# A second norm applied in two places, its feature weights by quarter beside the output products and its token factor at scores and Gelu

## The chip, the cores and the metric

The program runs on one core of one Trainium2 chip. The metric is the time of one execution in microseconds on the device; lower is better. The kernel before was run three times: median 2408.66 us, from 2407.15 to 2410.4.

## What is computed

A stream `x` of 256 tokens by 1024 features goes through one block with a conventional feed-forward part and then through two layers of a second kind. The change is in those two layers only. One such layer is:

```python
def rms_norm_2(x, g):
    y = xf * lax.rsqrt(jnp.mean(xf * xf, axis=-1, keepdims=True) + EPS)
    return (y * g.astype(jnp.float32)).astype(x.dtype)

x = x + token_mixer(rms_norm_2(x, norm_mix[l]), ...)      # ends with merged @ w_out
x = x + peer_ffn(rms_norm_2(x, norm_ffn[l]), ...)

def chunk(xc):                                             # in peer_ffn
    q = (xc @ w_query).reshape(PEER_CHUNK, PEER_HEADS, 2, half)
    s = jnp.einsum('thpk,pnk->thpn', q, sub_keys)
    sv, si = lax.top_k(s, PEER_TOPK)
...
    g = jax.nn.softmax(top_s, axis=-1)
    u = expert_down[eidx]
    vv = expert_up[eidx]
    act = jax.nn.gelu(jnp.einsum('td,thkd->thk', xc, u), approximate=False)
    return jnp.einsum('thk,thkd->td', (g * act), vv)
```

The normed stream `xc` is used twice: in the query product, whose result is scored against 128 keys per side, and in the dot products with 128 chosen expert rows per token (8 heads, 16 each). Both uses are linear in it up to the scores and up to the Gelu.

## The kernel before, in words

**Products.** All weights stream through a ring of three slots (`weights`, L884 on SyncE's queue), in halves of 512 KB. A half is split into a high part by ScalarE (`split_hi`, L443) and a low part by VectorE (`split_lo`, L448); the features are split likewise (`feat_hi`, `feat_lo`, called FH and FL). A product is then three matmuls (`product`, L463 to L465). `split_hi` of half n + 3 waits until half n's products are done (`half_done`), and the load of a slot waits for `split_lo` of what was in it. One half is eight products, 24 matmuls; a group is two halves and 256 output columns.

**The layers of the second kind** are a loop of two turns on each engine, with the instructions written in the same order on each turn. After attention and the two branch products come the four groups of output products (`wo_pe`, WO = 4). Their eight halves stand in the order `WO_ORDER`: group 0 and 1 first by feature half, then groups 2 and 3. I number these halves 0 to 7. As each group is done, VectorE adds it to its quarter of the stream `x` (L1501).

**The norm before the queries** (`n_peer`) then runs as a chain over four engines. ScalarE loads the table with the root (L316) and sums the squares of the first three quarters (`squares_act`, L324), then of the last (`norm_act`, L335), and takes the root (L340). VectorE forms mean and reciprocal (L348, L352, L356) and multiplies the stream by token factor and feature weights into `h_norm`, called HN (L366). TensorE, which runs 28 products with zeros meanwhile to stay busy (`keep_warm(pe, 7)`, L403), transposes HN in 16 blocks (`norm_pe`, L410); ScalarE copies each bank to FH (L390), VectorE subtracts to FL (L373).

**The queries and keys.** Eight query groups follow (`group_fm`, L_PQ = 8), each copied by ScalarE to `pqT` (L1294) and scored (`key_scores`, L1064); ScalarE copies the scores of one head to `SC` in one instruction (`take_scores`, L1286). VectorE finds the top 16 of 16 by pieces: `keyed` and `paired`, for the first head written between the weight splits of the query groups, up to the indices (L1569).

**The experts.** POOL issues a gather of 1 MB for each of 256 picks per layer into a ring of eight slots (L930). For each, VectorE takes the dot product with HN (L1612), ScalarE takes Gelu (L1313), multiplies by the gate (L1315) and forms a diagonal (L1318), and TensorE accumulates (L1085) and frees the slot.

What sets the order around the change is each engine's written order alone, with these semaphores: `half_done`, `wo_taken` (a bank of output products is read), `x_ready`, and of the norm `hn` (HN ready), `xp` (transposed), `hi` and `hT` (feature parts ready).

## Time and profile before

| | |
|---|---|
| median of 3 runs | 2408.66 us |
| profiled execution | 2412.3 us |
| its span, first to last instruction | 2410.5 us |
| granted TensorE clock, mean | 0.98 |
| TensorE busy | 2107.4 us (87%) |
| VectorE busy | 1640.8 us (68%) |
| ScalarE busy | 1113.4 us (46%) |
| POOL busy | 822.3 us (34%) |
| read from memory | 708.29 MB, 296 GB/s over the span |

The profiled execution is one more run than the three, with 1.8 us around its span. Busy time is a mean over stages that have different limits, so the stage has to be looked at: output products, norm and query products of layer 1 lie between 765 and 855 us, its gathers between 841 and 1490; in layer 2 the same begins near 1680. Of each wait the profile names the engine and line that released it.

### The profile page before, as it was taken

What the parts mean: (1) busy time and instruction counts of PE and PEld (TensorE: products, weight loads), DVE (VectorE), ACT (ScalarE), POOL (GpSimd) and SP (SyncE); (2) the same over time, 40 slices, a digit from 0 to 9 for tenths busy, and PEclk for the clock granted to TensorE, in tenths of its full rate; (3) what the DMA queues carried; (4) which work ended last, traced back from release to release, by engine and by line L of the source; (5) the groups of instructions that cost most, each with busy time, mean ns of one, the idle gap of its engine ahead of it and who ended that gap; (6) DMA issues with size and microseconds to landing.
All of it is one profiled execution on the core that took longest, in us unless ns stands there. A gap on an engine that the chain in (4) does not pass through costs nothing.

```text
span 2410.5 us, 32536 instructions
## 1 busy us (share of the span) xinstructions
PE 2107.4 (87%) x10192; PEld 1383.8 (57%) x10246; DVE 1640.8 (68%) x3313; ACT 1113.4 (46%) x2532; POOL 822.3 (34%) x562
## 2 busy tenths in 40 slices
PE   8999999999999988878877787999987877878877
PEld 7899899998999842222322222999852222322222
DVE  3555777777766577777777775776567777777776
ACT  5344455555544444444444444544444444444443
POOL 0000011100100066655666662010056566665663
PEclk9999999999999999999999998999999999999999
DMA  7333456655533499999999997433489999999998
GB/s 257 123 116 126 143 163 196 204 190 188 166 109 130 132 420 422 422 422 422 421 421 422 422 422 317 167 114 110 136 349 422 422 422 422 422 422 422 422 422 345
DMA packets 122844, 710.66 MB, mean 295 GB/s; under 512 B 14161, under 2 KB 16721, under 8 KB 56582
## 3 DMA queue, kind: packets, MB, share of 16 engines
q0 software_dynamic: 75264, 540.05, 54.1%
q1 hardware_dynamic: 43600, 159.12, 20.0%
q10 hardware_dynamic: 3894, 10.35, 1.2%
q8 instruction: 54, 0.88, 0.2%
q14 instruction: 32, 0.26, 0.0%
HBM read 708.29 MB, written 4.32 MB: 296 GB/s over the span
## 4 chain that ended last, share of the span: by engine, by line
PE 46%; DMA 31%; issue 7%; ACT 6%; DVE 5%; POOL 5%; POOLq 0%; ACTq 0%; DVEq 0%
DMA work<-in_experts,expert_idx 31%; PE ps L463 11%; PE ps L465 11%; PE ps L464 11%; PE ps L1085 6%; POOL work L930 5%; DVE work L1612 2%; PE ps L543 2%; PE ps L578 2%; PE ps L556 1%; ACT arena L1318 1%; ACT small L1315 1%; ACT L1313 1%; DVE weights_lo L448 1%; PE ps L1064 1%
## 5 line engine op out<-in xcount | busy, mean ns | idle before, releaser
L1085 PE MATMUL ps<-work,arena 128*128 128x512 f32 x2048 | 1017.2, 629 | 250.5 <-ACT arena L1318 248.9
L930 POOL DMA_INDIRECT work<-in_experts,expert_idx x512 | 778.9, 1521 | 843.7 <-issue 554.6
L1085 PEld LDWEIGHTS ps<-work,arena 128*128 128x128 f32 x2048 | 365.9, 194 | 900.1 <-ACT arena L1318 592.5
L1612 DVE CUSTOM_DVE_ANT_0 work<-h_norm,work 128x1024 f32<-128x1024 f32 x512 | 629.9, 1230 | 338.5 <-DMA work<-in_experts,expert_idx 332.0
L448 DVE TENSOR_TENSOR weights_lo<-weights,weights_hi 128x1024 fp32r<-128x1024 f32 x298 | 367.2, 1237 | 220.6 <-ACT weights_hi L443 220.4
L443 ACT ACTIVATE weights_hi<-weights 128x1024 fp32r<-128x1024 f32 x298 | 314.3, 1057 | 383.5 <-PE ps L465 363.8
L463 PE MATMUL ps<-feat_hi,weights_hi 128*128 128x256 f32 x1576 | 452.8, 287 | 7.6 <-DVE feat_lo L376 4.1
L464 PE MATMUL ps<-feat_lo,weights_hi 128*128 128x256 f32 x1576 | 447.5, 284 | 0.0
L465 PE MATMUL ps<-feat_hi,weights_lo 128*128 128x256 f32 x1576 | 447.3, 284 | 0.0
L1313 ACT ACTIVATE small<-small 128x1 f32<-128x1 f32 x512 | 103.7, 203 | 666.8 <-DVE small L1612 666.2
L463 PEld LDWEIGHTS ps<-feat_hi,weights_hi 128*128 128x128 f32 x1576 | 304.1, 193 | 12.1 <-issue 7.2
L464 PEld LDWEIGHTS ps<-feat_lo,weights_hi 128*128 128x128 f32 x1576 | 304.3, 193 | 0.6
L465 PEld LDWEIGHTS ps<-feat_hi,weights_lo 128*128 128x128 f32 x1576 | 303.9, 193 | 0.0
L1318 ACT ACTIVATE arena<-consts,small 128x128 f32<-128x128 f32 x512 | 205.6, 402 | 16.7
L904 POOL DMA_DIRECT2D na_rows<-in_rpb x32 | 21.2, 662 | 467.0 <-PE ps L465 467.0
L463 PE MATMUL ps<-weights_hi,feat_hi 128*128 128x256 f32 (+1 forms) x560 | 164.3, 293 | 7.0 <-DVE feat_lo L749 5.3
L1315 ACT ACTIVATE small<-small,expert_gate 128x1 f32<-128x1 f32 x512 | 150.7, 294 | 16.6
L464 PE MATMUL ps<-weights_lo,feat_hi 128*128 128x256 f32 (+1 forms) x560 | 158.2, 282 | 0.0
L465 PE MATMUL ps<-weights_hi,feat_lo 128*128 128x256 f32 (+1 forms) x560 | 158.0, 282 | 0.0
L463 PEld LDWEIGHTS ps<-weights_hi,feat_hi 128*128 128x128 f32 x560 | 107.4, 192 | 8.3 <-issue 4.4
L464 PEld LDWEIGHTS ps<-weights_lo,feat_hi 128*128 128x128 f32 x560 | 107.2, 191 | 0.7
L465 PEld LDWEIGHTS ps<-weights_hi,feat_lo 128*128 128x128 f32 x560 | 107.2, 191 | 0.0
(174 smaller groups left out, 1785.1 us busy)
## 6 DMA issues: line engine op xcount, KB each, us to landing
weights<-in_wstream SPq DMA_DIRECT2D x298, 512.0 KB, 3.6
work<-in_experts,expert_idx POOLq DMA_INDIRECT x512
na_rows<-in_rpb POOLq DMA_DIRECT2D x32, 96.0 KB, 4.0
arena<-na_rows ACTq DMA_DIRECT2D x2, 1536.0 KB, 10.7
params<-in_par ACTq DMA_DIRECT2D x2, 1476.0 KB, 7.3
work<-bias_rows ACTq DMA_DIRECT2D x3, 512.0 KB, 6.6
params<-in_par ACTq DMA_DIRECT2D x1, 1156.0 KB, 11.7
x<-in_x SPq DMA_DIRECT2D x1, 1024.0 KB, 5.0
```

The costliest lines, as they stand in the source:

```text
L443: nc.scalar.activation(WH[:, n % SLOTS, :], W[:, n % SLOTS, :], ACT.Copy).then_inc(w_hi, 1)
L448: nc.vector.tensor_tensor(WL[:, n % SLOTS, :], W[:, n % SLOTS, :], WH[:, n % SLOTS, :], ALU.subtract).then_inc(w_lo, 1)
L463: nc.tensor.matmul(out, stat[0], mov[0], start=start, stop=False)
L464: nc.tensor.matmul(out, stat[0], mov[1], start=False, stop=False)
L465: return nc.tensor.matmul(out, stat[1], mov[0], start=False, stop=stop)
L543: ins = nc.tensor.matmul(ps[:, at:at + k.shape[-1]], q, k, start=True, stop=True)
L930: nc.gpsimd.indirect_dma_start(ring[:, r, :], None, experts, bass.IndirectOffsetOnAxis(ap=EIDX[:, b, c * RING + r:c * RING + r + 1], axis= ...
L1085: ins = nc.tensor.matmul(bank(2 * t + h), DIAG[:, r, :], ring[:, r, D + h * 512:D + (h + 1) * 512], start=False, stop=False)
L1313: nc.scalar.activation(ga[:, r:r + 1], hd[:, r:r + 1], ACT.Gelu).then_inc(gelu_ready, 1)
L1315: nc.scalar.activation(gw8[:, r:r + 1], ga[:, r:r + 1], ACT.Copy, scale=GWT[:, b, c * RING + r:c * RING + r + 1]).then_inc(w_ready, 1)
L1318: nc.scalar.activation(DIAG[:, r, :], ident, ACT.Copy, scale=gw8[:, r:r + 1]).then_inc(diag_ready, 1)
L1612: nc.vector.tensor_tensor_reduce(ring[:, r, 0:D], HN[:, t, :], ring[:, r, 0:D], 1.0, 0.0, ALU.mult, ALU.add, hd[:, r:r + 1]).then_inc(dots ...
```

## The change

In the loop of the two layers, the norm's two factors are taken apart. The feature weights are multiplied in by VectorE quarter by quarter, right after each quarter of the sum (so HN is now the stream times the feature weights, without the token factor). TensorE transposes quarters 0, 1 and 2 after halves 4, 5 and 6 of the output products, and quarter 3 inside the first query half, after its fourth chunk; the keep-warm products and `norm_pe` go. ScalarE copies the transposed banks 0 and 1 after half 6 and banks 2 and 3 after half 7, since FH and FL still hold the merged features until then. The squares are summed over whole rows afterwards, into `Y` instead of HN; root and reciprocal follow. The token factor `rstd` enters as a per-token scale when the scores are copied (now one instruction per 128 tokens, L1313 of the changed kernel) and as the scale of Gelu.

```diff
--- before.py
+++ after.py
@@ -759,7 +759,15 @@
             split_lo(dve, 2 * (g0 + BR) - 1 + SLOTS, at)
             lower(BR - 1)
 
-        def wo_pe(pe, gates, g0, l=0, at=0):
+        def turned_pe(pe, nm, l, g):
+
+            pe.wait_ge(nm.hn, 4 * l + g + 1)
+            for c in (2 * g, 2 * g + 1):
+                for t in range(TT):
+                    ins = nc.tensor.transpose(ps[:, c * S + t * P:c * S + (t + 1) * P], HN[:, t, c * P:(c + 1) * P], ident)
+            ins.then_inc(nm.xp, 1)
+
+        def wo_pe(pe, gates, g0, l=0, at=0, turned=None):
 
 
             done = 0 if isinstance(l, int) else l * BR + BR
@@ -770,6 +778,8 @@
                     pe.wait_ge(wo_taken, g - 1 if isinstance(l, int) else l * (WO - 1) + WO + g - 1)
                 half_tok(pe, 2 * g0 + n, 6 + g % 2, h, at,
                          also=(lambda c: c % 2 or pe.wait_ge(mt_lo, done + c // 2 + 1)) if g == 0 else None)
+                if turned and n in (4, 5, 6):
+                    turned_pe(pe, turned, l, n - 4)
 
         def wo_done(g):
 
@@ -1049,10 +1059,7 @@
                     else:
                         values_pe(pe, AT2, what[1], l)
                 branches_pe(pe, AT2, fill_o2, G_LAYER + LG_BR, PARTS2, l, at)
-                wo_pe(pe, (lproj_taken, l * N2 + L_PROJ + L_GATE), G_LAYER + LG_WO, l, at)
-
-                keep_warm(pe, 7)
-                norm_pe(pe, n_peer, l)
+                wo_pe(pe, (lproj_taken, l * N2 + L_PROJ + L_GATE), G_LAYER + LG_WO, l, at, turned=n_peer)
 
                 def key_scores(h):
 
@@ -1066,11 +1073,17 @@
                                                    PAR[:, Q_KEYS + s * NKEY:Q_KEYS + (s + 1) * NKEY], start=True, stop=True)
                     ins.then_inc(sc_done, 1)
 
+                def normed(c):
+
+                    if c == 4:
+                        turned_pe(pe, n_peer, l, 3)
+                    if c % 2 == 0:
+                        pe.wait_ge(n_peer.hT, l * 4 + c // 2 + 1)
+
                 for j in range(L_PQ):
                     if j >= 2:
                         pe.wait_ge(lproj_taken, l * N2 + L_PROJ + L_GATE + j - 1)
-                    group_fm(pe, G_LAYER + LG_PQ + j, 6 + j % 2, at, also=(
-                        lambda c: c % 2 or pe.wait_ge(n_peer.hT, l * 4 + c // 2 + 1)) if j == 0 else None)
+                    group_fm(pe, G_LAYER + LG_PQ + j, 6 + j % 2, at, also=normed if j == 0 else None)
                     if j != 1:
                         key_scores(max(j - 1, 0))
                 key_scores(PH - 1)
@@ -1268,13 +1281,25 @@
                         heads_parts(nc.scalar, AT2, what[1].fill + what[1].copies, l, range(EARLY))
                 gates_act(2 * KC, (lproj_taken, l * N2 + L_PROJ + L_GATE))
                 merge_act(act, AT2, fill_o2, G_LAYER + LG_BR, l, at)
-                for n in range(2 * LG_WO, 2 * LG_PQ):
-                    split_hi(act, L_HALF + n + SLOTS, at)
-                root_table(303)
-                squares_act(act, stream, (wo_taken, l * (WO - 1) + WO + WO - 1))
+                wo_halves = at.halves + L_HALF + 2 * LG_WO
+                for n in range(2 * WO - 2):
+                    split_hi(act, L_HALF + 2 * LG_WO + n + SLOTS, at)
+                    if n == 3:
+                        root_table(303)
+                for b in range(4):
+                    if b in (0, 2):
+                        act.wait_ge(half_done, wo_halves + 2 * WO - 1 + b // 2)
+                    act.wait_ge(n_peer.xp, 4 * l + b + 1)
+                    nc.scalar.activation(two(FH, b), bank(b), ACT.Copy).then_inc(n_peer.hi, 1)
+                    if b == 1:
+                        split_hi(act, L_HALF + 2 * LG_PQ + 1, at)
+                split_hi(act, L_HALF + 2 * LG_PQ + 2, at)
                 act.wait_ge(x_ready, l * 3 + 2 * TT + 1)
-                norm_act(act, n_peer, stream, l, first=EARLY_D)
-                norm_act_hi(act, n_peer, l, None)
+                for t in range(TT):
+                    ins = nc.scalar.activation(Y[:, t, :], X[:, t, :], ACT.Square, accum_out=ssq[:, t:t + 1])
+                ins.then_inc(n_peer.sq, 1)
+                act.wait_ge(n_peer.var, l + 1)
+                nc.scalar.activation(std, ssq, ACT.Sqrt).then_inc(n_peer.std, 1)
 
                 def gate_exp(k):
 
@@ -1283,8 +1308,11 @@
 
                 def take_scores(h):
                     act.wait_ge(sc_done, l * PH + h + 1)
-                    nc.scalar.activation(SC[:, 0:STEPS, :, :].rearrange("p (t h) s n -> p t h (s n)", h=PH)[:, :, h, :],
-                                         bank(4 + h % 2).rearrange("p (t n) -> p t n", t=TT), ACT.Copy).then_inc(sc_ready, 1)
+                    act.wait_ge(n_peer.rstd, l + 1)
+                    for t in range(TT):
+                        ins = nc.scalar.activation(SC[:, t * PH + h, :, :].rearrange("p s n -> p (s n)"),
+                                                   bank(4 + h % 2)[:, t * 2 * NKEY:(t + 1) * 2 * NKEY], ACT.Copy, scale=rstd[:, t:t + 1])
+                    ins.then_inc(sc_ready, 1)
 
                 for j in range(L_PQ):
                     n = 2 * (LG_PQ + j) + SLOTS
@@ -1310,7 +1338,7 @@
                                 for r in range(RING):
                                     pick = l * PICKED + k * TOPK + (c * RING + r + 1)
                                     act.wait_ge(dots_ready, pick)
-                                    nc.scalar.activation(ga[:, r:r + 1], hd[:, r:r + 1], ACT.Gelu).then_inc(gelu_ready, 1)
+                                    nc.scalar.activation(ga[:, r:r + 1], hd[:, r:r + 1], ACT.Gelu, scale=rstd[:, t:t + 1]).then_inc(gelu_ready, 1)
                                     act.wait_ge(gelu_ready, pick)
                                     nc.scalar.activation(gw8[:, r:r + 1], ga[:, r:r + 1], ACT.Copy,
                                                          scale=GWT[:, b, c * RING + r:c * RING + r + 1]).then_inc(w_ready, 1)
@@ -1494,14 +1522,33 @@
                     elif what[0] == "V":
                         heads_dve(dve, ch, AT2, what[1], l)
                 merge_dve(dve, ch, AT2, fill_o2, G_LAYER + LG_BR, 2, (gates_on, l + 2), l, at)
+                def lower(b):
+
+                    dve.wait_ge(n_peer.hi, 4 * l + b + 1)
+                    nc.vector.tensor_tensor(two(FL, b), bank(b), two(FH, b), ALU.subtract).then_inc(n_peer.hT, 1)
+
                 for g in range(WO):
-                    los(LG_WO + g)
+                    if g < WO - 1:
+                        los(LG_WO + g)
+                    else:
+                        lower(0)
+                        lower(1)
                     dve.wait_ge(half_done, at.halves + L_HALF + 2 * LG_WO + wo_done(g))
                     dst = X[:, :, g * GC:(g + 1) * GC]
                     ins = nc.vector.tensor_tensor(dst, dst, bank(6 + g % 2).rearrange("p (t n) -> p t n", t=TT), ALU.add)
-                    ins.then_inc(wo_taken if g < WO - 1 else x_ready, 1)
-                dve.wait_ge(x_ready, l * 3 + 2 * TT + 1)
-                norm_dve_pre(dve, n_peer, l, None, PAR[:, Q_GF:Q_GF + D], split=l * TT + 2 * TT)
+                    if g < WO - 1:
+                        ins.then_inc(wo_taken, 1)
+                        dve.wait_ge(wo_taken, l * (WO - 1) + WO + g + 1)
+                    else:
+                        ins.then_inc(x_ready, 1)
+                        dve.wait_ge(x_ready, l * 3 + 2 * TT + 1)
+                    nc.vector.tensor_tensor(HN[:, :, g * GC:(g + 1) * GC], dst,
+                                            view(PAR[:, Q_GF + g * GC:Q_GF + (g + 1) * GC], [0, TT], [1, GC]), ALU.mult).then_inc(n_peer.hn, 1)
+                lower(2)
+                lower(3)
+                split_lo(dve, L_HALF + 2 * LG_PQ + 1, at)
+                split_lo(dve, L_HALF + 2 * LG_PQ + 2, at)
+                norm_dve_rstd(dve, n_peer, l)
 
                 def keyed(rc, k):
```

**Order on TensorE.** First place, the end of the output products and the first query group, before (L463 to L465 are products, L403 keep-warm, L410 transposes, L452 the step of the weights' semaphore):

```order
L465 MATMUL ps<-weights_hi,feat_lo 128x256
L401 UNCONDITIONAL_BRANCH
L403 MATMUL ps<-zero 128x512 x4
L401 REGISTER_ALU
L401 COMPARE_AND_BRANCH
L410 MATMUL ps<-consts,h_norm 128x128 x16
L452 REGISTER_ALU
L463 MATMUL ps<-feat_hi,weights_hi 128x256
```

Now the same place, from the fourth chunk of the first query half on (L767 are the transposes):

```order
L463 MATMUL ps<-feat_hi,weights_hi 128x256
L464 MATMUL ps<-feat_lo,weights_hi 128x256
L465 MATMUL ps<-feat_hi,weights_lo 128x256
L767 MATMUL ps<-consts,h_norm 128x128 x4
L463 MATMUL ps<-feat_hi,weights_hi 128x256
```

The sixteen transposes and the keep-warm loop between the two kinds of products are gone; four transposes stand after twelve query products, and the other twelve, four each, after output halves 4, 5 and 6.

**Order on VectorE.** Second place, from the last output group's sum into the stream to the first scores, before (L448 are low parts of weights, L1501 the sum, L366 the multiplies, L373 low parts of features):

```order
L448 TENSOR_TENSOR weights_lo<-weights,weights_hi 128x1024
L1501 TENSOR_TENSOR x<-x,ps 128x2x256
L1503 REGISTER_ALU
L347 REGISTER_ALU
L348 TENSOR_SCALAR small<-small 128x2
L352 SCALAR_TENSOR_TENSOR small<-small 128x2
L356 RECIPROCAL small<-small 128x2
L366 SCALAR_TENSOR_TENSOR h_norm<-x,small,params 128x1024 x2
L373 TENSOR_TENSOR feat_lo<-ps,feat_hi 128x512 x4
L1580 MEMSET arena 128x512
```

Now (L1538 is the sum, L1545 the multiply by feature weights, L1528 the low parts of features):

```order
L1528 TENSOR_TENSOR feat_lo<-ps,feat_hi 128x512 x2
L1538 TENSOR_TENSOR x<-x,ps 128x2x256
L1545 TENSOR_TENSOR h_norm<-x,params 128x2x256
L1528 TENSOR_TENSOR feat_lo<-ps,feat_hi 128x512 x2
L447 REGISTER_ALU
L448 TENSOR_TENSOR weights_lo<-weights,weights_hi 128x1024
L447 REGISTER_ALU
L448 TENSOR_TENSOR weights_lo<-weights,weights_hi 128x1024
L354 TENSOR_SCALAR small<-small 128x2
L356 RECIPROCAL small<-small 128x2
L1627 MEMSET arena 128x512
```

Two low parts of weights moved from before the sum to behind the feature parts, the two 1024-wide multiplies became one small one after each sum, and the mean and reciprocal stand last.

## Rows read from the trace of the kernel before

**Rows 1.** Page, part 4: the chain that ended last, by engine.
```profile
PE 46%; DMA 31%; issue 7%; ACT 6%; DVE 5%; POOL 5%; POOLq 0%; ACTq 0%; DVEq 0%
```

**Rows 2.** Stretches in us: length, busy time (instructions) of each engine, clock granted, DMA.
```profile
806.00:840.00 34.00, 33.35 (x281) 33.35 (x282) 21.41 (x51) 17.50 (x24) 0.00 (x0) 1.00 0.47 157
...
870.00:1480.00 610.00, 489.01 (x989) 175.23 (x987) 440.37 (x1117) 267.17 (x798) 373.83 (x244) 0.98 1.01 422
```

**Rows 3.** Chain of waits, layer 1: start us, length us, what.
```profile
788.15 0.13 PE ps L465
...
789.38 1.28 ACT L316
...
790.78 1.74 ACT h_norm L324 x4
792.52 0.81 ACT h_norm L335 x4
...
794.06 2.49 DVE h_norm L366 x2
...
796.59 3.53 PE ps L410 x16
```

**Rows 4.** The same chain, first key scores of layer 1, both ends in layer 2.
```profile
806.65 1.16 PE ps L1064 x8
...
1702.88 0.13 PE ps L465
...
1721.37 1.16 PE ps L1064 x8
```

**Rows 5.** Timelines of VectorE and POOL: start, length, engine, line, tiles; wait ahead in brackets.
```profile
837.48 1.23 DVE L448 TENSOR_TENSOR weights_lo<-weights,weights_hi 128x1024 fp32r<-128x1024 f32 x1 [2.05 <-ACT weights_hi L443]
...
839.61 0.23 DVE L1569 TENSOR_SCALAR expert_idx<-arena,small 128x16 uint32<-128x16 f32 x1
...
840.98 2.02 POOL L930 DMA_INDIRECT work<-in_experts,expert_idx  x1 [178.42 <-issue]
```

**Rows 6.** Groups by line, VectorE, 870 to 1480: busy us, mean ns, idle before.
```profile
L1612 DVE CUSTOM_DVE_ANT_0 work<-h_norm,work 128x1024 f32<-128x1024 f32 x245 | 301.6, 1231 | 162.2 <-DMA work<-in_experts,expert_idx 160.2 <-issue 0.3
```

**Rows 7.** Timeline of TensorE where attention values meet the branch products.
```profile
741.10 1.09 PE L556 MATMUL ps<-consts,work 128*128 128x128 f32 x8 [0.78 <-DVE work L615]
741.95 0.36 PE L463 MATMUL ps<-feat_hi,weights_hi 128*128 128x256 f32 x1
742.15 0.28 PE L464 MATMUL ps<-feat_lo,weights_hi 128*128 128x256 f32 x1
```

**Rows 8.** Groups by line and shape, ScalarE then VectorE; one row of ScalarE's timeline.
```profile
L443 ACT ACTIVATE weights_hi<-weights 128x1024 fp32r<-128x1024 f32 x298 | 314.3, 1057 | 383.5 <-PE ps L465 363.8 <-DMA weights<-in_wstream 19.2 <-ACT work L1103 0.4
L1318 ACT ACTIVATE arena<-consts,small 128x128 f32<-128x128 f32 x512 | 205.6, 402 | 16.7
L1315 ACT ACTIVATE small<-small,expert_gate 128x1 f32<-128x1 f32 x512 | 150.7, 294 | 16.6
L1313 ACT ACTIVATE small<-small 128x1 f32<-128x1 f32 x512 | 103.7, 203 | 666.8 <-DVE small L1612 666.2
...
L393 ACT ACTIVATE feat_hi<-ps,params 128x256 fp32r<-128x256 f32 x32 | 12.1, 489 | 4.8 <-PE ps L410 4.8
...
L448 DVE TENSOR_TENSOR weights_lo<-weights,weights_hi 128x1024 fp32r<-128x1024 f32 x298 | 367.2, 1237 | 220.6 <-ACT weights_hi L443 220.4
...
L742 DVE TENSOR_TENSOR work<-work 128x512 f32<-128x512 f32 x16 | 11.1, 692 | 0.5
...
819.35 0.60 ACT L1294 ACTIVATE arena<-ps 128x512 f32<-128x512 f32 x1 [1.82 <-PE ps L465]
```

**Rows 9.** Stretches around waits of TensorE, columns as in rows 2.
```profile
762.00:764.00 2.00, 0.74 (x7) 0.64 (x6) 0.88 (x2) 1.14 (x3) 0.00 (x0) 1.00 0.38 96
...
794.00:796.00 2.00, 0.32 (x2) 0.00 (x0) 1.97 (x3) 0.00 (x0) 0.00 (x0) 1.00 0.00 0
...
798.00:799.00 1.00, 1.00 (x6) 1.00 (x6) 0.69 (x1) 0.74 (x2) 0.00 (x0) 0.50 0.00 0
```

## The prediction

> **What bounds the kernel now.** I read the summary of the chain that ended last, then the table of stretches for layer 1, then the chain through the norm in both layers, and last the mean times of single instructions. The chain is 46% TensorE and 31% DMA [rows 1]. The reader should see in it that no one engine bounds this program: it alternates between stretches of products and stretches of expert gathers. In the query products TensorE is busy 33.35 of 34 us at full clock (281 products, 0.12 us apart, so 2.88 us for a half group of 24); in the gathers the DMA engines are at a share of 1.01 with 422 GB/s while TensorE waits [rows 2].
>
> Between the output products and the query products lies the norm. The chain shows it as one line without cover: the last output product starts at 788.15, then come the table load (1.28), the squares (1.74 and 0.81), root and reciprocal, the two 1024-wide multiplies (2.49 together) and 16 transposes (3.53) [rows 3]. The first key scores start at 806.65, and in layer 2 the same points lie at 1702.88 and 1721.37: 18.50 and 18.49 us [rows 4]. Two half groups need only 5.76 of these. That is where the change acts, twice.
>
> **Does a gain there reach the end?** The first gather starts at 840.98, 1.1 us after VectorE's indices are ready (839.61 + 0.23). VectorE's work for those indices is interleaved with weight splits which wait for ScalarE, and through it for TensorE's finished halves: 2.05 us of waiting before the split at 837.48 [rows 5]. So the indices come at TensorE's pace and move with it. From then on VectorE waits for gathers (160.2 us in the stretch [rows 6]) and 256 gathers of 1.05 MB (128 rows of 2048 fp32 numbers) need about 640 us at 422 GB/s, 2.48 each, whatever precedes them. A microsecond saved ahead of the query products should therefore be one microsecond at the end.
>
> **The change, part by part, for one layer.** I let t = 0 be the end of the last output product.
>
> Transposes between the output products. Twelve of the sixteen now stand there. Eight transposes between attention values and branch products took 0.85 us until the next product started, 0.106 each, and that product shows 0.36 us where the next shows 0.28 [rows 7]. So +1.28 us, and +0.08 for each of four returns to products, 0.3. The third quarter waits: its feature weights come after a weight split that ScalarE can only begin once half 5 is done. From the end of half 5: hop 0.15, high part 1.06, low part 1.23, sum into the stream 0.69, multiply 0.69 (the two 128x512 ones as the one of that size in [rows 8], which also has the weights' parts), about 3.85 with the overlaps and hops; TensorE has by then four transposes (0.43), a product with zeros (about 0.2) and half 6 (2.88) behind it, 3.5 us. I take a wait of 0.4. Sum ahead of t = 0: **+1.7**, and 0.3 for the returns.
>
> The first query group. VectorE's chain from t = 0 is sum 0.69, multiply 0.69 and two hops: the last quarter is ready at 1.6. TensorE meanwhile has quarters 0 and 1 (ScalarE and VectorE split them under the last output half: 2 x 0.60 and 2 x 0.69 inside 2.88 us) and does 12 products, to 1.44. Four transposes end at 2.05; ScalarE's copy takes 0.60, VectorE's difference 0.69, with hops 3.65, and in between TensorE has two chunks (0.72). The last two chunks end at 4.4. The second half needs its weights' low part, 1.23, which VectorE does only after that difference: 4.85. It ends at 7.7. Then ScalarE's copy of the queries as before, 0.67: key scores at **8.4**, where they are now at 18.37 (18.50 less one product of 0.13). Saved 10.0, less 1.7 and 0.3: **8.0 us per layer**.
>
> The root. It leaves the path: squares over all of X (two passes of 1024, 1.06 each as the weights' high part [rows 8]), root and reciprocal run on ScalarE and VectorE beside the first group and end near t = 6.6. Behind them on ScalarE is queued a weight split of 1.06, then the copy of the queries; they end at 7.65, just when TensorE finishes, so this costs nothing, and 0.5 if a hop more is in it. The scores wait for the reciprocal only after that. What would go wrong if this cover were gone is a delay of key scores one for one.
>
> The scores' factor. One copy of 128x512 (0.60) becomes two of 128x256 with a per-token factor, 0.489 each as the nearest such row: +0.3 with their overlap [rows 8]. ScalarE waits 1.82 us for TensorE ahead of a copy in this loop [rows 8], so nothing; only the last head's copy delays the first Gelu by 0.3. The gather that waits for it, the ninth, has eight in hand, 8 x 2.48 us from 841, so until 861 at the earliest and later with the last three weight halves (another 1.5 MB) among them. Nothing.
>
> Gelu's factor, 512 times. The trace has no Gelu with a factor from memory. Below it is bounded by Gelu as it is, 0.203 (+0), above by the 128x1 copy with one, 0.294 (+0.09) [rows 8]; I take +0.09, since only the operand differs. ScalarE's three instructions for a pick (Gelu, gate, diagonal 0.402 [rows 8]) are then 0.99 of the 2.48 us a pick has. Hidden by the DMA engines; perhaps 0.1 us at each layer's end. If the loop over the eight ring slots were bound by latency, each of its 64 turns would grow by 0.09, 5.8 us in all. POOL's and SP's queues get no new instruction, and no DMA moves past another.
>
> Keep-warm products. Twenty-eight disappear per layer; the work they bridged is gone.
>
> **Sum.** 2 x 8.0 = 16.0 us off the profiled execution (2412.3, span 2410.5): 2396.3. The median of the runs, 2408.66, is 3.6 lower; from it the forecast is **2392.7**. With every hand-over free, at most 10.2 per layer could be saved (18.50 - 0.13 - 0.67 = 17.7 from product to copy, less 5.76 and 1.7), 2388.3, which bounds it on the fast side.
>
> A rule that speaks against the change: in the rows, transposes run at 0.106 us and the clock stays full around them [rows 7]. The Trainium skill (TensorE: Matmul & The Clock Gate, Part 4: PE-mode transpose) gives about 275 ns for a transpose in a kernel's context and says it doesn't count as TensorE activity in the usual way. By that figure an estimate of the saving is 2.7 us less per layer; the spacing in the trace disagrees with it for runs of four to eight.
>
> **Rivals.**
> 1. The hand-overs cost more. Each of four interruptions makes TensorE wait about 0.7 us more than I counted (late multiply, late low part, the root before the copy of the queries): 2 x 2.8 lost, 10.4 saved: 2398.3. For it: five cross-engine hops where there was one chain, and ScalarE's slack at the first group is 0.05. Against: each duration above has a row.
> 2. The longer Gelu is not hidden: 16.0 - 5.8 = 10.2 saved, 2398.5. Against it is the wait of VectorE for gathers [rows 6].
> 3. The time comes back before the gathers: 2408.7. If the first indices were bound by VectorE's own chain rather than by TensorE's halves, an earlier first score would not bring them forward. The 2.05 us waits speak against it [rows 5].
> 4. Slower: the clock. The trace grants TensorE 1.00 where it is idle for 1.26 of 2 us (762 to 764). Where it is idle for 1.68 of the 2 us after the keep-warm products and until 796.59, 2.27 in all, it still has 1.00 and then falls to 0.50, the 1.2 GHz level, at 798 [rows 9]. The keep-warm products go, and waits and transposes come in their place. At 1.2 GHz work takes double, so 16 us spent at that level undo the 8.0 of a layer; if all query products (16 halves of 2.88) ran so, it would be +46 - 8 per layer: 2485. Against it: my longest wait is 0.5 us, and products fill the rest. The same page of the Trainium skill (Part 1) says the low level is where an idle array falls; by that rule too this needs an idle stretch, which I do not find.
> 5. The change does not do what it says: the order of instructions shows the transposes between the products and the 16-fold run gone, so I give this nothing of its own.
>
> **How the numbers follow.** A measurement of this kernel can tell about 0.2%, 4.8 us, from no change. Forecast 0.82; rival 1 0.06; rival 2 0.05; rival 3 0.04; rival 4 0.03. The first three are faster by more than 4.8: 0.93. Within 0.2%: 0.04. Slower: 0.03. The range goes from 2389, the forecast with nearly free hand-overs, to 2400, past rivals 1 and 2.
>
> **What would show it.** In the profile after, the time from the last output product to the first key score is about 8.4 us plus one product, in both layers, with no wait of TensorE over 0.6; output products stretch by about 2.0; the clock stays 1.00 across the passage; the first gather starts near 833 and the last stretch of gathers is as long as before at 422 GB/s; Gelu takes 0.29. I am wrong if the first gather does not move by what the first key score moved, if the granted clock falls near 790, or if gathers show a share below 1.

## The result, and the profile after

The changed kernel takes 2394.82 us (median of four runs, 2394.11 to 2397.05) where the kernel before takes 2409.11 (median of four): a ratio of 0.9941, with 0.9925 to 0.9957 as its 95% interval. A second comparison (run e5 below) gave 2394.68 against 2410.79, 0.9935 [0.9921, 0.9948]. The medians differ by 14.3 and 16.1 us, and the intervals allow 10 to 19; 16.0 was forecast. The forecast of the time itself was 2392.7, so the median is 2.1 us above it, inside the range of 2389 to 2400.

| | before | after |
|---|---|---|
| profiled execution, us | 2412.3 | 2397.05 |
| its span, us | 2410.5 | 2395.3 |
| first output product to last one's end, layer 1 | 23.92 | 25.65 |
| end of last output product to first key scores, layer 1 | 18.37 | 8.52 |
| first key scores to first gather, layer 1 | 34.33 | 34.45 |
| first gather to first gather of layer 2 | 914.64 | 907.51 |

The chain that ended last, by engine, in the page of the changed kernel:

```profile
PE 45%; DMA 21%; POOL 14%; issue 10%; ACT 6%; DVE 5%; ACTq 0%; POOLq 0%; DVEq 0%
```

Against [rows 1] the share of DMA fell from 31% to 21% and that of POOL rose from 5% to 14%. The shift goes with the longer Gelu: in run e1 below, which takes the factor out of Gelu and nothing else, the chain is again

```profile
PE 46%; DMA 32%; issue 6%; DVE 6%; ACT 5%; POOL 4%; POOLq 0%; ACTq 0%; DVEq 0%; SPq 0%
```

POOL's mean time to issue one gather moves with it: 1521 ns before, 1638 with the change, 1524 in e1. I had not foreseen this, and why it happens is open. It did not show in the length of the gathers: first gather to the end of layer 1 takes 649.3 us before, 649.2 with the change and 649.1 in e1. The lengths of the stretches say more than the shares of the chain.

The passage from the output products to the first query group, and the gathers of layer 1, in stretches (length in us, busy time and instructions of each engine, granted clock, DMA share, GB/s):

```profile
786.00:788.00 2.00, 1.79 (x15) 1.59 (x15) 1.49 (x3) 1.49 (x3) 0.00 (x0) 1.00 0.67 242
...
792.00:794.00 2.00, 1.51 (x11) 1.12 (x10) 1.22 (x3) 1.58 (x3) 0.00 (x0) 1.00 0.00 0
...
798.00:800.00 2.00, 1.31 (x12) 1.25 (x12) 0.75 (x1) 1.60 (x3) 0.00 (x0) 1.00 0.74 229
...
864.00:1470.00 606.00, 484.86 (x979) 173.92 (x977) 436.77 (x1112) 287.71 (x794) 398.96 (x242) 0.98 1.01 422
```

Where TensorE was busy 0.32 of 2 us at 794 and had a granted clock of 0.50 at 798 [rows 9], it is now busy at least 1.31 of each 2 us from 786 to 806, and the clock is 1.00 in each of these slices. The gathers run at the same 422 GB/s, the same share of 1.01 and the same mean clock of 0.98 as in [rows 2].

The chain of waits through the same passage (start, length, what); it answers to [rows 3]:

```profile
785.22 0.69 DVE x L1538
...
785.94 0.70 DVE h_norm L1545
...
786.69 0.66 PE ps L767 x4
...
790.10 0.13 PE ps L465
...
790.26 0.70 DVE x L1538
...
790.98 0.70 DVE h_norm L1545
...
791.72 0.67 PE ps L767 x4
792.42 0.61 ACT feat_hi L1293
...
793.05 0.05 DVE feat_lo L1528
...
793.66 1.22 DVE weights_lo L448
...
794.92 0.39 PE ps L463
...
798.10 0.60 ACT arena L1322
...
798.75 1.16 PE ps L1071 x8
```

The last output product ends at 790.23, and 0.03 later VectorE sums the last quarter. Table load, squares, root and the two 1024-wide multiplies of [rows 3] are gone from the chain. What is left is sum, multiply, four transposes, the two feature parts, the low part of the second half's weights, and that half. In each row below the bracket gives TensorE's wait ahead of it, with the engine and line that ended it:

```profile
786.69 0.66 PE L767 MATMUL ps<-consts,h_norm 128*128 128x128 f32 x4 [0.21 <-DVE h_norm L1545]
...
793.79 0.39 PE L463 MATMUL ps<-feat_hi,weights_hi 128*128 128x256 f32 x1 [0.49 <-DVE feat_lo L1528]
...
794.92 0.39 PE L463 MATMUL ps<-feat_hi,weights_hi 128*128 128x256 f32 x1 [0.15 <-DVE weights_lo L448]
...
798.75 0.49 PE L1071 MATMUL ps<-params,arena 128*128 128x128 f32 x2 [0.69 <-ACT arena L1322]
```

ScalarE beside them, then VectorE's indices and POOL's first gather (start, length, engine, line, and in brackets the idle time ahead), against [rows 5]:

```profile
796.43 1.06 ACT L443 ACTIVATE weights_hi<-weights 128x1024 fp32r<-128x1024 f32 x1
798.10 0.60 ACT L1322 ACTIVATE arena<-ps 128x512 f32<-128x512 f32 x1 [0.60 <-PE ps L465]
```

```profile
831.83 0.23 DVE L1616 TENSOR_SCALAR expert_idx<-arena,small 128x16 uint32<-128x16 f32 x1
```

```profile
833.20 1.90 POOL L940 DMA_INDIRECT work<-in_experts,expert_idx  x1 [170.40 <-issue]
```

ScalarE has 0.60 us in hand ahead of the copy of the queries. The first gather starts at 833.20 rather than 840.98.

The groups that the token factor touches (busy us, mean ns, idle before), against [rows 8]:

```profile
L1343 ACT ACTIVATE small<-small,expert_gate 128x1 f32<-128x1 f32 x512 | 150.7, 294 | 16.7
L1341 ACT ACTIVATE small<-small 128x1 f32<-128x1 f32 x512 | 150.1, 293 | 621.1 <-DVE small L1659 620.5
...
L1313 ACT ACTIVATE arena<-ps,small 128x256 f32<-128x256 f32 x32 | 13.3, 470 | 2.2 <-PE ps L1071 2.2
```

The Gelu took 203 ns and takes 293. It adds 46 us of busy time to ScalarE in 512 picks, and ScalarE waits 621 us in all ahead of it.

### The profile page after: what moved, and what is told of

It is laid out like the page before. It is cut to its first block, busy times and chain, and to the rows that moved or that the text cites. A ratio compares the mean times of both kernels' runs of the same rounds, so it can differ in the third digit from the quotient of the medians.

```text
span 2395.3 us, 32478 instructions
## 1 busy us (share of the span) xinstructions
PE 2091.7 (87%) x10190; PEld 1374.0 (57%) x10190; DVE 1638.7 (68%) x3315; ACT 1161.6 (48%) x2540; POOL 881.9 (37%) x562
## 4 chain that ended last, share of the span: by engine, by line
PE 45%; DMA 21%; POOL 14%; issue 10%; ACT 6%; DVE 5%; ACTq 0%; POOLq 0%; DVEq 0%
DMA work<-in_experts,expert_idx 21%; POOL work L940 14%; PE ps L463 11%; PE ps L464 11%; PE ps L465 11%; PE ps L1098 4%; PE ps L543 2%; PE ps L578 2%; DVE work L1659 2%; PE ps L556 1%; ACT L1341 1%; DVE weights_lo L448 1%; ACT L1307 1%; ACT arena L1346 1%; PE ps L1071 1%
## 5 line engine op out<-in xcount | busy, mean ns | idle before, releaser
L940 POOL DMA_INDIRECT work<-in_experts,expert_idx x512 | 838.5, 1638 | 765.7 <-issue 516.0
L448 DVE TENSOR_TENSOR weights_lo<-weights,weights_hi 128x1024 fp32r<-128x1024 f32 x298 | 367.1, 1238 | 208.6 <-ACT weights_hi L443 208.5
L463 PE MATMUL ps<-feat_hi,weights_hi 128*128 128x256 f32 x1576 | 453.9, 288 | 8.8 <-DVE feat_lo L376 4.0
L1341 ACT ACTIVATE small<-small 128x1 f32<-128x1 f32 x512 | 150.1, 293 | 621.1 <-DVE small L1659 620.5
L465 PE MATMUL ps<-feat_hi,weights_lo 128*128 128x256 f32 x1576 | 448.4, 284 | 0.0
L463 PEld LDWEIGHTS ps<-feat_hi,weights_hi 128*128 128x128 f32 x1576 | 304.1, 193 | 14.5 <-issue 7.1
L465 PEld LDWEIGHTS ps<-feat_hi,weights_lo 128*128 128x128 f32 x1576 | 304.0, 193 | 0.0
L463 PE MATMUL ps<-weights_hi,feat_hi 128*128 128x256 f32 (+1 forms) x560 | 165.0, 295 | 6.3 <-DVE feat_lo L749 4.6
L465 PE MATMUL ps<-weights_hi,feat_lo 128*128 128x256 f32 (+1 forms) x560 | 158.5, 283 | 0.0
L463 PEld LDWEIGHTS ps<-weights_hi,feat_hi 128*128 128x128 f32 x560 | 107.6, 192 | 8.3 <-issue 4.4
L926 POOL TENSOR_TENSOR work<-arena,consts 128x640 f32<-128x640 f32 x8 | 13.8, 1756 | 256.3 <-DVE arena L1493 256.3
```

What stands on the lines that cost most here:

```text
L448: nc.vector.tensor_tensor(WL[:, n % SLOTS, :], W[:, n % SLOTS, :], WH[:, n % SLOTS, :], ALU.subtract).then_inc(w_lo, 1)
L463: nc.tensor.matmul(out, stat[0], mov[0], start=start, stop=False)
L465: return nc.tensor.matmul(out, stat[1], mov[0], start=False, stop=stop)
L940: nc.gpsimd.indirect_dma_start(ring[:, r, :], None, experts, bass.IndirectOffsetOnAxis(ap=EIDX[:, b, c * RING + r:c * RING + r + 1], axis= ...
L1341: nc.scalar.activation(ga[:, r:r + 1], hd[:, r:r + 1], ACT.Gelu, scale=rstd[:, t:t + 1]).then_inc(gelu_ready, 1)
```

## The experiments

In the tables below the distances are of layer 1, from the start of the first of the 192 output products that the trace lists (the two layers agree within 0.1 us, but for e4, where the first distance is 42.90 in layer 2). The kernel before beside e1 to e4 has a median of 2410.37, beside e5 to e8 2410.79.

| kernel | first output product to first key scores | first key scores to first gather | median, us | ratio to before |
|---|---|---|---|---|
| before | 42.29 | 34.33 | 2409.11 | |
| the change | 34.17 | 34.45 | 2394.82 | 0.9941 [0.9925, 0.9957] |
| e1, Gelu without the factor | 34.17 | 34.45 | 2394.89 | 0.9939 [0.9922, 0.9955] |
| e2, transposes after the products | 34.74 | 34.45 | 2396.18 | 0.9945 [0.9928, 0.9961] |
| e3, keep-warm products back | 39.90 | 34.46 | 2406.37 | 0.9986 [0.9977, 0.9996] |
| e4, before without keep-warm | 43.08 | 34.32 | 2411.57 | 1.0004 [0.9994, 1.0013] |
| e5, the change again | 34.15 | 34.44 | 2394.68 | 0.9935 [0.9921, 0.9948] |
| e6, a low part earlier | 33.75 | 34.44 | 2393.79 | 0.9926 [0.9912, 0.9939] |
| e7, e6 and indices earlier | 33.74 | 31.05 | 2393.20 | 0.9927 [0.9913, 0.9940] |
| e8, e7 and waits filled | 33.44 | 31.06 | 2393.75 | 0.9921 [0.9908, 0.9935] |

**e1: is the longer Gelu hidden?**

```diff
-nc.scalar.activation(ga[:, r:r + 1], hd[:, r:r + 1], ACT.Gelu, scale=rstd[:, t:t + 1]).then_inc(gelu_ready, 1)
+nc.scalar.activation(ga[:, r:r + 1], hd[:, r:r + 1], ACT.Gelu).then_inc(gelu_ready, 1)
```

> The changed kernel with Gelu again without its scale (the token factor is missing in the dot products, so the output differs; scores keep it). Theory A, the gathers are bound by the DMA engines and hide ScalarE's longer pick: Gelu falls from 0.293 to 0.203 us, the time stays at 2394.8 within 1 us, first gather to end of layer 1 stays at 649.3 us. Rival B, each of the 64 turns of the slot ring carries the 0.09 us: 5.8 us less, 2389.

Its group row:

```profile
L1341 ACT ACTIVATE small<-small 128x1 f32<-128x1 f32 x512 | 103.7, 203 | 665.8 <-DVE small L1659 665.1
```

The Gelu is back at 203 ns, and the 46 us reappear as 45 us more of waiting for VectorE's dot products. The median is 2394.89, the same as with the factor. From the first gather to the end of layer 1 it takes 649.1 us, against 649.2 with the factor, where rival B's 32 turns per layer would have taken off 2.9. The longer Gelu is hidden, and rival 2 falls.

**e2: which part earns the gain?** The twelve transposes of quarters 0 to 2 stand in one run behind the output products; the last four stay inside the first query half, and the root stays off the path.

```diff
-                wo_pe(pe, (lproj_taken, l * N2 + L_PROJ + L_GATE), G_LAYER + LG_WO, l, at, turned=n_peer)
+                wo_pe(pe, (lproj_taken, l * N2 + L_PROJ + L_GATE), G_LAYER + LG_WO, l, at)
+                for g in range(3):
+                    turned_pe(pe, n_peer, l, g)
```

> The changed kernel with the twelve transposes of quarters 0 to 2 after all output products instead of between them. Theory A: the output products shorten by 1.7 us per layer, but the feature parts of quarters 0 and 1 now stand ahead of the last sum on VectorE, so the last quarter is ready near t = 4.0 instead of 1.5 and the key scores start near t = 10.8 instead of 8.5: per layer +0.5, in all 2395.8, so nearly the whole gain comes from taking the token factor off the path and only about 0.5 us per layer from putting transposes beside output products. Rival: the wait of about 2 us right after the output products drops the granted clock to 1.2 GHz in the first query group, up to 3 us more per layer, 2402. Rival C, the transposes beside the output products carry the gain: 8 us per layer lost again, 2410.

TensorE's timeline, and the stretch in which it is idle most:

```profile
787.62 1.47 PE L767 MATMUL ps<-consts,h_norm 128*128 128x128 f32 x12
789.78 0.36 PE L463 MATMUL ps<-feat_hi,weights_hi 128*128 128x256 f32 x1 [0.69 <-DVE feat_lo L1530]
```

```profile
788.00:790.00 2.00, 1.31 (x12) 1.10 (x11) 1.05 (x2) 1.69 (x3) 0.00 (x0) 1.00 0.00 0
```

Only 0.57 us per layer is lost. The transposes cost nearly the same in either place; what is lost is mainly the wait of 0.69 for the feature parts, which the output products cover otherwise. So the placing of the twelve transposes gives 0.57 of the 8.12 us per layer, and 7.55 come from all the rest together: the squares, the root and the token-wise multiplies off the path, the first query products that run before the last quarter is ready, and the clock. No run takes these apart. For the clock an estimate is possible: the sixteen transposes of the kernel before took 3.53 us [rows 3] at a granted clock of 0.50 [rows 9], and at e2's 0.12 each they would take 1.9, so some 1.6 us. The difference of the medians, 1.4 us, is no more than the runs scatter; the distance is what shows the 0.57.

**e3: does a microsecond on the path carry to the end?** The keep-warm products come back behind the changed output products.

```diff
                 wo_pe(pe, (lproj_taken, l * N2 + L_PROJ + L_GATE), G_LAYER + LG_WO, l, at, turned=n_peer)
+                keep_warm(pe, 7)
```

> The changed kernel with the 28 keep-warm products put back between output and query products: a known delay on TensorE of 6.0 us, of which about 1.5 lie over waits that are there anyway. Theory A (what TensorE loses ahead of the key scores is lost at the end, one for one): key scores later by 4.2 to 4.6 us per layer, the first gather by as much, in all 8.4 to 9.2 us more, 2403.2 to 2404.0. Rival C (the gathers absorb shifts): the first gather moves by less than 2 us per layer.

```profile
789.60 5.99 PE L403 MATMUL ps<-zero 128*128 128x512 bf16 x21
795.24 0.47 PE L463 MATMUL ps<-feat_hi,weights_hi 128*128 128x256 f32 x1
...
798.87 0.38 PE L463 MATMUL ps<-feat_hi,weights_hi 128*128 128x256 f32 x1 [0.70 <-DVE feat_lo L1529]
...
800.00 0.39 PE L463 MATMUL ps<-feat_hi,weights_hi 128*128 128x256 f32 x1 [0.16 <-DVE weights_lo L448]
...
803.81 1.16 PE L1072 MATMUL ps<-params,arena 128*128 128x128 f32 x8 [0.69 <-ACT arena L1323]
```

(The profile lists 21 of the 28.) The first key scores come 5.73 us later, where 4.2 to 4.6 was expected: a miss. I had counted on the delay to swallow the waits of the first group, but those (0.70, 0.16, 0.69) follow TensorE's own fourth run of transposes and its own last product; they move along and stay. The point of the run is in the rest: the first gather is later by 5.74 relative to the same first product, and from there the two stretches of gathers are as long as in the change (layer 1 649.2 us in both, layer 2 648.4 against 648.3), so nothing is absorbed and rival C falls. The median is 11.48 above e1's, which ran beside it on the same chip. That this is just twice 5.74 is luck, since e3's ten runs reach from 2402.4 to 2411.1 and e1's four from 2392.1 to 2396.0; within some 4 us, delay on this path reaches the end one for one.

**e4: what does the clock cost?** The kernel before, without the keep-warm products ahead of its second norm.

```diff
-                keep_warm(pe, 7)
                 norm_pe(pe, n_peer, l)
```

> The kernel before with its keep-warm products ahead of the second norm removed: 8.3 us of idle TensorE. Theory A: the granted clock is 0.50 from 796.6 on and returns later than before (there at about 800.3), a first query group in part at 1.2 GHz, 1 to 2 us more per layer: 2411 to 2413. Rival: nothing, as the transposes ran at 0.50 before as well and TensorE waits for the feature parts anyway: 2409.

```profile
796.22 3.67 PE L410 MATMUL ps<-consts,h_norm 128*128 128x128 f32 x16 [8.32 <-DVE h_norm L366]
```

```profile
790.00:792.00 2.00, 0.00 (x0) 0.00 (x0) 0.84 (x2) 1.99 (x6) 0.00 (x0) 0.81 0.33 72
792.00:794.00 2.00, 0.00 (x0) 0.00 (x0) 0.81 (x4) 1.15 (x7) 0.00 (x0) 0.50 0.52 203
...
800.00:801.00 1.00, 1.00 (x7) 1.00 (x7) 0.84 (x2) 0.53 (x1) 0.00 (x0) 0.50 0.00 0
801.00:802.00 1.00, 1.00 (x8) 1.00 (x8) 0.74 (x2) 0.00 (x0) 0.00 (x0) 0.77 0.00 0
```

TensorE is idle for 8.32 us, the clock falls to 0.50 (the level of 1.2 GHz), and work that starts at 796.22 runs at 0.50 until inside 801 to 802 (the 0.77 there puts the return near 801.5). In the kernel before it was at 0.50 too [rows 9], and came back sooner:

```profile
800.00:801.00 1.00, 1.00 (x9) 1.00 (x9) 0.84 (x2) 0.60 (x1) 0.00 (x0) 0.90 0.00 0
```

Counted from the first output product, TensorE works at 0.50 some 1.6 us longer in layer 1 of e4, and half of that, 0.8, is what work at half speed loses. Measured are 0.79 us in layer 1 and 0.62 in layer 2, under the 1 to 2 expected, and the medians agree within the measurement. So the 28 keep-warm products of the kernel before bought some 0.7 us per layer; they had not prevented the fall. Taking them out gains nothing by itself; in the change they can go because the gap that they stood in is closed. The run does not price a clock that never falls, as it is at 0.50 in both kernels.

**e5: the change again**, on the chip of e6 to e8, so that these four share their runs of the kernel before.

> The changed kernel itself once more, beside the three below on one chip, so that they have a base: 2394.8 within 1.5 us, 0.994 of the kernel before.

The ratio is 0.9935 [0.9921, 0.9948] and the median within 0.2 us of the first; the distances are those of the first profile within 0.02 us.

**e6: a late low part earlier.** The wait ahead of 794.92 above is for the low part of the second half's weights, which VectorE makes only after the last feature part. VectorE has been idle 1.83 us under the last output half; there the low part fits.

```diff
                         lower(1)
+                        split_lo(dve, L_HALF + 2 * LG_PQ + 1, at)
...
                 lower(3)
-                split_lo(dve, L_HALF + 2 * LG_PQ + 1, at)
                 split_lo(dve, L_HALF + 2 * LG_PQ + 2, at)
```

> The low part of the second query half's weights moved into VectorE's 1.8 us of idle time under the last output half. Theory A: TensorE's 0.42 us between the first two query halves goes, key scores 0.4 us earlier per layer, 0.8 us in all, hardly seen in the time but seen in the trace. Rival: ScalarE's chain (squares, root, weight split, copy of the queries), which has 0.5 us to spare, takes its place and less than 0.2 is left.

```profile
793.77 0.39 PE L463 MATMUL ps<-feat_hi,weights_hi 128*128 128x256 f32 x1 [0.49 <-DVE feat_lo L1528]
798.32 0.94 PE L1071 MATMUL ps<-params,arena 128*128 128x128 f32 x6 [0.69 <-ACT arena L1322]
```

The wait at 794.92 is gone, and from the start of the last output product that the trace lists to the first key scores it is 8.40 us instead of 8.82, in both layers. That is the full 0.42, so the rival, ScalarE's chain, falls. That the 0.84 us reach the median (2393.79 against 2394.68) cannot be told from scatter.

**e7: the indices earlier.** On VectorE they stood behind the low part of half 13 of the query weights; now they stand behind that of half 12. In the loop that mixes low parts with the search for the best keys:

```diff
-                        for m in range(nxt, min(nxt + 2, L_HALVES)):
+                        step = 1 if n == 9 else 2
+                        for m in range(nxt, nxt + step):
                             split_lo(dve, L_HALF + m, at)
-                        nxt += 2
+                        nxt += step
```

> As the one before, and the first head's indices no longer stand behind the low part of weights half 13 of the queries but behind half 12. Theory A (the first gather comes when TensorE's pace of halves lets VectorE get to the indices, and everything behind it is as long as the DMA engines take): first gather about 3.1 us earlier relative to the key scores (31.3 instead of 34.4), and 3.1 per layer at the end: 2394.8 - 0.8 - 6.2 = 2387.8. Rival D: the ring of eight slots is full before the first slot is freed (ninth gather waits for the first accumulation, which does not move), the DMA engines go idle between, and nothing or under 1 us per layer comes through: 2392 to 2394. Rival E: the early gathers delay the last weight halves and TensorE waits for them: later last key scores.

POOL's first and ninth gather of layer 1, and then a stretch of DMA in e6 and the same one in e7:

```profile
829.37 2.04 POOL L940 DMA_INDIRECT work<-in_experts,expert_idx  x1 [166.57 <-issue]
...
852.19 0.97 POOL L940 DMA_INDIRECT work<-in_experts,expert_idx  x1 [10.63 <-PE ps L1098]
```

```profile
832.00:836.00 4.00, 4.00 (x36) 4.00 (x35) 1.44 (x2) 2.27 (x4) 2.88 (x2) 1.00 0.55 184
```

```profile
832.00:836.00 4.00, 4.00 (x36) 4.00 (x35) 1.43 (x2) 2.27 (x4) 3.19 (x3) 1.00 0.99 399
```

The first gather comes 3.4 us earlier, and the end barely moves (2393.20 against e6's 2393.79): theory A, 2387.8, misses, and the time is where rival D put it, 2392 to 2394.

In layer 1 the first eight gathers only fill DMA time that is free. In e6 the engines are at 0.55 in these 4 us and at 1.03 from 836 on, so the transfers can win about 0.45 x 4 = 1.8 us. Layer 1 ends 2.2 us earlier than e6's (1479.73 against 1481.94). That is not a gain to count on: e8 below starts its gathers as early and ends layer 1 at 1481.86.

In layer 2 nothing of the 3.4 us is left by the last gathers, and here it is rival D that the trace shows. These are the ninth gather of layer 2 in e7 and two stretches of DMA around and behind it:

```profile
1758.15 1.04 POOL L940 DMA_INDIRECT work<-in_experts,expert_idx  x1 [13.67 <-PE ps L1098]
```

```profile
1745.28:1757.28 12.00, 9.14 (x49) 6.51 (x48) 11.58 (x31) 8.06 (x21) 0.00 (x0) 0.82 0.93 390
1757.28:1797.28 40.00, 35.98 (x77) 13.80 (x75) 26.17 (x69) 17.84 (x51) 25.50 (x19) 0.97 0.94 377
```

All eight slots are filled, POOL waits 13.67 us for TensorE's first accumulation (8.54 in e6), and meanwhile the DMA engines run dry: 0.93 and 0.94 where e6 has 1.01 in the same two stretches, which is 0.08 x 12 + 0.07 x 40 = 3.8 us of their time. Most of it lies between 1753.45 and 1761.45, where the share is 0.72 and then 0.40. e8 shows the same fall there, with a wait of 14.05. In layer 1 the wait is 10.63 (9.28 in e6) and the share stays at 0.99 or more; why the two layers differ is open. The change itself met neither limit: it moved the loads of the query weights together with the gathers (the DMA share in slices of 4 us reads 0.42, 0.38, 0.52, 1.04 from 832 before and 0.45, 0.41, 0.52, 1.01 from 824 with the change) and the first accumulation with them (857.93 and 849.84).

**e8: the rest of the waits filled.** The first query group's two halves are interleaved, so that the second half's first four chunks run while the last feature quarter is made.

```diff
-                    group_fm(pe, G_LAYER + LG_PQ + j, 6 + j % 2, at, also=normed if j == 0 else None)
+                    if j == 0:
+                        first_queries()
+                    else:
+                        group_fm(pe, G_LAYER + LG_PQ + j, 6 + j % 2, at)
...
+                    for h, c in [(0, c) for c in range(6)] + [(1, c) for c in range(4)] + [(0, 6), (0, 7)] + [(1, c) for c in range(4, 8)]:
```

> As the one before, and the first query group starts its second half on the first four chunks while the last quarter is turned and split, with one more product with zeros to open the bank. Theory A: the 0.49 us wait of TensorE for the last feature parts goes, less 0.2 for the product with zeros, but ScalarE's chain to the copy of the queries then ends last: key scores 0.3 us earlier per layer than in the one before, 2387.2.

Another 0.31 us of the path goes (8.09 from the start of the last output product to the first key scores), as expected. The time is not: 2393.75, where 2387.2 was expected from e7's figure. The runs reach from 2387.49 to 2396.33, a scatter that hides 0.3 us per layer. All three variants have medians about 1 us under the change's; none is clear of it.

## Why the prediction was right, step by step

**Output products, +1.7 and +0.3.** They stretched by 1.73 (1.72 in layer 2), 2.0 predicted. The term that was too large is the wait of the third quarter, 0.4: it is 0.21. The rest, 1.52, is close to what twelve transposes (1.28) and the returns (0.3) were counted at. In e2 the twelve stand in one run and take 1.47 us, 0.12 each, and the clock stays 1.00. The Trainium skill (TensorE: Matmul & The Clock Gate, Part 4: PE-mode transpose) gives about 275 ns for one. The trace agrees with that as the duration of a single one: the 32 of L767 have a median of 273 ns. But they are pipelined and follow each other at 0.12 us, and the spacing is what a run of them costs. The prediction set the page's duration against the spacing of [rows 7] and called it a disagreement; there is none, and its estimate of 2.7 us less does not follow.

**The first query group, key scores at 8.4.** They start 8.52 after the last output product's end (8.82 after its start as the timeline lists it). The marks on the way, predicted and measured from t = 0 at 790.23: transposes of the last quarter 1.6 and 1.49; next product after the feature parts 3.65 and 3.56; second half 4.85 and 4.69; its end 7.7 and 7.85. The last took 3.16 us where 2.88 was counted, since the first product behind a wait takes 0.39 until its result, not 0.12. Saved 9.85 rather than 10.0. The prediction's sign of no wait over 0.6 fails by the letter: TensorE waits 0.69 ahead of the key scores. That is ScalarE's copy of the queries, which the sum had at 0.67.

**Net, 8.0 per layer.** 9.85 - 1.73 = 8.12. Rival 1, hand-overs at 0.7 more each, would have left 5.2 of it; it falls. Two small misses cancel here, 0.27 too much for the output products and 0.12 too little for the query group, so the net is closer than its parts.

**The root.** It does leave the path. Its slack was put at 0.05; it is 0.60, because ScalarE's split ended at 7.26, not 7.65, and TensorE's products at 7.85, not 7.7. The reader should take from this that the forecast was closer than the knowledge behind it: a root 0.7 us later would have shown.

**The scores' factor.** Per pair 0.84 us instead of 0.60 (two of 0.47 with their overlap), +0.24 where +0.3 was put, and probably not quite hidden: the first gather is 0.12 us later against the first key scores, in both layers, which I had put at nothing. No run has the single copy back, so that the 0.12 is the factor's is not shown.

**Gelu.** +0.09 as put, hidden (e1). Its side effect on POOL's issues was not in the prediction.

**Carry-through.** One to one, for the change (first gather 7.78 earlier: 8.12, less 0.12, less 0.22 by which the output products began later) and in e3. Rival 3 falls. The argument against it, VectorE's waits at the split [rows 5], is right for this change, but the premise that 256 gathers need about 640 us whatever precedes them is too simple: in e7, where the gathers start earlier and the loads and the first accumulation do not, the gathers of layer 2 take 652.5 us against e6's 648.0.

**The clock.** 1.00 through the whole passage; rival 4 falls. The sum had no term for the clock; what its fall had cost the kernel before is inside the measured 18.37 us, so the gain of closing the gap came along unnamed.

**The total.** 2 x (8.12 - 0.12) = 16.0, less 0.22 at the start. The profiled execution went from 2412.3 to 2397.05, by 15.2; 16.0 was predicted. The remaining 0.5 lies between the first gather and layer 2 (+0.9, mostly the turn of the layer loop, below) and behind the first gather of layer 2 (-0.3). The medians differ by 14.3 and 16.1 in the two comparisons. That the profiled execution came within 0.8 us of the forecast is in part luck, as the turn of the loop alone differs by more than 3 us between profiles. No step of the sum failed in kind.

## What to carry to other kernels

A norm's token factor can be moved behind a linear step, so that the products need only feature weights, which come piece by piece; count first how long the squares, root and multiplies stand alone on the chain, and whether the clock falls behind them, because that, and not the placing of the transposes, is most of the gain (7.55 of 8.12 us here). Whether an earlier start of a transfer-bound stretch pays depends on what the DMA engines would do in the time won, and on whether the buffers last until the first of them is freed: it paid in full where the loads ahead and the first accumulation moved as well, and hardly at all (e7) where gathers alone did. For terms under a microsecond compare distances between two marks of the profile, here reproducible to 0.02 us, rather than whole times, whose runs scatter by 2 to 9 us.

## What the runs showed that I had not expected

At the turn of the layer loop TensorE is idle for a time that differs from run to run of kernels that are the same there. Its timeline in the kernel before, the changed one, the same kernel again (e5), and e1; for the wait in brackets no releaser is named:

```profile
1498.47 1.86 PE L403 MATMUL ps<-zero 128*128 128x512 bf16 x4 [5.48 <-issue]
```

```profile
1491.29 6.72 PE L403 MATMUL ps<-zero 128*128 128x512 bf16 x18 [5.87 <-issue]
```

```profile
1489.18 6.36 PE L403 MATMUL ps<-zero 128*128 128x512 bf16 x18 [3.95 <-issue]
```

```profile
1487.29 6.81 PE L403 MATMUL ps<-zero 128*128 128x512 bf16 x18 [2.86 <-issue]
```

The wait is 5.87 and 3.95 us in two runs of the same kernel, and 2.86 in e1; from the end of layer 1 to the first output product of layer 2 it is 189.8 us in the changed kernel's profile and 186.4 in e1's. That is as large as the scatter of the changed kernel's runs, and likely a good part of it. In each case it lies in a stretch in which loads keep the DMA engines busy (a share of 0.91 to 0.99); whether they cause it was not tried.

The keep-warm products were worth less than the fall suggests: without them TensorE idles 8.32 us and works about 5 us at 0.50, but with them it worked at 0.50 too, for about 3.6 us, so only the difference, 0.7 us per layer, is theirs.
